# A gate group's projection as products over both parts of u, with its additions inside a softmax step and some steps moved

## The reference, cut to what matters

```
u    = modulate(rms_norm(x), shift, scale)
proj = u @ w_in            # split into q_m k_m v_m o_m if_m | q_a k_a v_a | g_m g_a
h_m  = sigmoid(o_m) * norm(mlstm(silu(conv(q_m, k_m)), v_m, gates))
h_a  = dilated window attention with ALiBi, 12 heads in 3 patterns, merged by softmax of log-sums
y    = sigmoid(g_m) * (h_m @ w_branch_m) + sigmoid(g_a) * (h_a @ w_branch_a)
x    = x + gate * (y @ w_out)
x    = x + gate * moe(...)     # 16 experts, top 2 of one group; then a final norm
```

## Time and profile before

| | us |
|---|---|
| median of 3 runs (lowest, highest) | 595.68 (595.04, 596.05) |
| the profiled execution, its own time | 594.85 |
| its span, first to last instruction | 593.1 |
| PE busy | 573.2 |
| DVE busy | 319.1 |
| ACT busy | 241.2 |

### The profile page before, as it was taken

How to read it: one execution, slowest core, us unless ns; L and a number is a source line. 1 busy time by engine, 2 the same in 40 slices (tenths; PEclk the granted TensorE clock), 3 DMA queues, 4 the chain that set the end, 5 groups by cost and what they waited for, 6 DMA issues and landing times.

```text
span 593.1 us, 8116 instructions
## 1 busy us (share of the span) xinstructions
PE 573.2 (97%) x3370; PEld 408.3 (69%) x3370; DVE 319.1 (54%) x487; ACT 241.2 (41%) x344; POOL 9.0 (2%) x23
## 2 busy tenths in 40 slices
PE   3999999999999999999999999999999999999995
PEld 1789978888888888999999988533534444353432
DVE  3679976776668868877847683612213030221204
ACT  5627658444455545764684335601111110111113
POOL 3001000000000000000000000000000000000000
PEclk9999999999999999999999999999999999999998
DMA  8999654666667939646688999399999999999992
GB/s 313 386 350 317 213 183 152 228 212 222 213 216 273 361 139 350 220 175 246 228 312 320 411 374 407 135 424 423 421 422 419 423 422 422 419 423 422 421 374 75
DMA packets 51577, 184.77 MB, mean 312 GB/s; under 512 B 3649, under 2 KB 3761, under 8 KB 37713
## 3 DMA queue, kind: packets, MB, share of 16 engines
q1 hardware_dynamic: 50706, 183.53, 80.3%
q10 hardware_dynamic: 704, 0.58, 0.3%
q0 software_dynamic: 128, 0.11, 0.1%
HBM read 183.16 MB, written 1.05 MB: 311 GB/s over the span
## 4 chain that ended last, share of the span: by engine, by line
PE 91%; DVE 4%; ACT 2%; DMA 1%; issue 1%; SPq 0%; ACTq 0%; DVEq 0%
PE ps L1660 20%; PE ps L1889 19%; PE ps L1682 15%; PE ps L1901 8%; PE ps L1637 8%; PE ps L1639 4%; PE ps L1935 3%; PE ps L1877 2%; DMA first_ada<-in_ada_w_dram 1%; PE ps L1911 1%; DVE lo L998 1%; PE ps L1671 1%; PE ps L1788 1%; PE ps L1773 1%; PE ps L1752 1%
## 5 line engine op out<-in xcount | busy, mean ns | idle before, releaser
L998 DVE TENSOR_TENSOR lo<-raw,hi 128x2048 fp32r<-128x2048 f32 (+1 forms) x51 | 114.4, 2249 | 38.6 <-ACT hi L641 38.2
L1889 PE MATMUL ps<-ring,xe_t 128*64 128x512 f32 x512 | 111.7, 593 | 0.0
L641 ACT CAST hi<-raw 128x2048 fp32r<-128x2048 f32 x50 | 95.0, 1912 | 30.1 <-PE ps L1660 15.6
L1889 PEld LDWEIGHTS ps<-ring,xe_t 128*64 128x64 f32 x512 | 36.5, 137 | 71.6 <-issue 71.4
L1660 PE MATMUL ps<-u_both,hi 128*128 128x256 f32 x448 | 82.1, 286 | 0.7 <-DVE lo L998 0.7
L1660 PEld LDWEIGHTS ps<-u_both,hi 128*128 128x128 f32 x448 | 69.9, 192 | 2.0 <-DVE lo L998 1.1
L1682 PE MATMUL ps<-hi,u_both 128*128 128x512 f32 x224 | 69.8, 393 | 1.3 <-DVE qk_m L1127 1.3
L1637 PE MATMUL ps<-u_both,hi 128*128 128x512 f32 x192 | 69.1, 403 | 0.0
L1660 PE MATMUL ps<-u_both,lo 128*128 128x256 f32 x224 | 63.5, 283 | 0.0
L1639 PE MATMUL ps<-u_both,lo 128*128 128x256 f32 x192 | 53.7, 280 | 0.0
L1457 DVE SCALAR_TENSOR_TENSOR he<-ps,w_slot,sg 128x512 f32<-128x512 f32 x8 | 6.0, 751 | 82.6 <-PE ps L1889 82.6
(11 more groups left out here) (350 smaller groups left out, 831.7 us busy)
## 6 DMA issues: line engine op xcount, KB each, us to landing
raw<-in_w_in_dram SPq DMA_DIRECT2D x41, 1024.0 KB, 5.4
ring<-in_w_gate_e_dram SPq DMA_DIRECT2D x32, 1024.0 KB, 17.3
ring<-in_w_up_e_dram SPq DMA_DIRECT2D x32, 1024.0 KB, 16.2
ring<-in_w_down_e_dram SPq DMA_DIRECT2D x28, 1024.0 KB, 15.8
raw<-in_ada_w_dram SPq DMA_DIRECT2D x16, 1024.0 KB, 6.0
first_ada<-in_ada_w_dram SPq DMA_DIRECT2D x16, 512.0 KB, 11.7
raw<-in_w_branch_m_dram SPq DMA_DIRECT2D x4, 1024.0 KB, 7.1
raw<-in_w_out_dram SPq DMA_DIRECT2D x4, 1024.0 KB, 9.2
```

The costliest lines, as they stand in the source:

```text
L641: nc.scalar.copy(hi[b % RING][:], src[:]).then_inc(hi_ready, 1)
L998: ins = V.tensor_tensor(lo[b % RING][:, tiles, :], src[:, tiles, :], hi[b % RING][:, tiles, :].bitcast(F32), ALU.subtract)
L1889: ins = mm(ps[bank][64 * s:64 * s + 64, :], xe_t[:, kk, col + s * SLOTS:col + (s + 1) * SLOTS], w[:, k, :], start=(kk == 0), stop=(kk == K ...
```

## The change

- WIDE takes in the kind gm (groups 17 and 18), with banks 0, 1 as its first pair. The sums go to `sig_gm`, and ACT's sigmoid then works in place there, after DVE's additions, where it read PSUM before.
- In the steps of gm (35 and 37) both pairs come ahead of the split of block s+2, on ACT and on DVE. For qa and ka the second pair stays behind it.
- Where the block before is one of SCORE_A_AT (block 35, after 34), DVE's additions of the first pair stand inside the softmax step of block 34, between a_max and the wait for a_exp. ACT's copies stay at the head of step 35.
- M_OUT_AT goes from 35 to 39.
- The adaLN pieces at 38 and 39 are gone; there are pieces at 17 and 21 instead, 16 in all as before.

```
--- before.py
+++ after.py
@@ -67,7 +67,7 @@
 NBLK = len(BLOCKS)
 BLK_IN = 2 * len(IN_GROUPS)
 AHEAD = RING - 1
-WIDE = [_g for _g, (_kind, _, _) in enumerate(GROUP_LIST) if _kind in ("qa", "ka")]
+WIDE = [_g for _g, (_kind, _, _) in enumerate(GROUP_LIST) if _kind in ("qa", "ka", "gm")]
 
 
 
@@ -80,7 +80,7 @@
 SCORE_A_AT = [28, 31, 34, 37]
 TURN_A_AT = [30, 33, 36, 39]
 VALUE_A_AT = [31, 34, 37, 40]
-M_OUT_AT = 35
+M_OUT_AT = 39
 M_TURN_AT = [BLK_IN - 2, BLK_IN - 1]
 FFN_ROWS_AT, FFN_COL_AT, SHIFT_LOGIT_AT = 43, 44, 45
 BCAST_AT = {45: 0}
@@ -89,7 +89,7 @@
 
 ADA_FIRST = 8
 ADA_REST = 16
-ADA_AT = {s: ADA_FIRST + i for i, s in enumerate([12, 14, 16, 18, 20, 22, 25, 26, 27, 29, 30, 32, 33, 36, 38, 39])}
+ADA_AT = {s: ADA_FIRST + i for i, s in enumerate([12, 14, 16, 17, 18, 20, 21, 22, 25, 26, 27, 29, 30, 32, 33, 36])}
 
 
 FIRST = ([("ada", a) for a in range(4)] + [("w", 0), ("w", 1), ("ada", 4), ("w", 2), ("ada", 5), ("ada", 6), ("ada", 7),
@@ -418,13 +418,13 @@
 
         def wide_banks(g):
 
-            return 2, 3, 0, 1
+            return (0, 1, 2, 3) if GROUP_LIST[g][0] == "gm" else (2, 3, 0, 1)
 
         def wide_out(g, c):
 
             kind = GROUP_LIST[g][0]
             j = [x for x in WIDE if GROUP_LIST[x][0] == kind].index(g)
-            return {"qa": q_a, "ka": k_a}[kind][:, 4 * j + c, :]
+            return {"qa": q_a, "ka": k_a, "gm": sig_gm}[kind][:, 4 * j + c, :]
 
         def wide_free(eng, g, pair):
 
@@ -705,14 +705,18 @@
 
             for s in range(NBLK):
                 g, _, _, end = BLOCKS[s]
+                kind, _, _ = GROUP_LIST[g]
                 if end and g in WIDE:
                     if g == WIDE[0]:
                         after(act, "u_lo1_3")
                     act.wait_ge(pair_done, WIDE.index(g) + 1)
                     copy_right(g, 0)
+                if end and kind == "gm":
+                    act.wait_ge(block_done, s + 1)
+                    copy_right(g, 1)
                 if s + AHEAD < NBLK and s + AHEAD != EARLY and s != LAST_BLOCK[24]:
                     split_hi(s + AHEAD)
-                if end and g in WIDE:
+                if end and g in WIDE and kind != "gm":
                     act.wait_ge(block_done, s + 1)
                     copy_right(g, 1)
                 if s == LAST_BLOCK[23]:
@@ -735,7 +739,10 @@
                 g, _, _, end = BLOCKS[s]
                 kind, _, _ = GROUP_LIST[g]
                 if end and evac_engine(g) == "act":
-                    act.wait_ge(block_done, s + 1)
+                    if g in WIDE:
+                        evacuated(act, g)
+                    else:
+                        act.wait_ge(block_done, s + 1)
                     first = min(x for x, (n, _, _) in enumerate(GROUP_LIST) if n == kind)
                     j = g - first
                     banks = banks_of(g)
@@ -755,7 +762,7 @@
                             view, src = dst[:, n, j * NB:(j + 1) * NB], ps[bank][:]
                         else:
                             view = dst[:, 4 * j + 2 * n:4 * j + 2 * n + 2, :]
-                            src = ps[bank][:].rearrange("p (c t) -> p c t", c=2)
+                            src = view if g in WIDE else ps[bank][:].rearrange("p (c t) -> p c t", c=2)
                         ins = A_(view, src, func)
                     ins.then_inc(evac_act, 1)
 
@@ -1105,11 +1112,14 @@
 
             for s in range(NBLK):
                 g, _, _, end = BLOCKS[s]
-                if end and g in WIDE:
+                kind, _, _ = GROUP_LIST[g]
+                if end and g in WIDE and s - 1 not in SCORE_A_AT:
                     add_halves(g, 0)
+                if end and kind == "gm":
+                    add_halves(g, 1)
                 if s + AHEAD < NBLK and s not in (1, LAST_BLOCK[24]):
                     split_lo(s + AHEAD)
-                if end and g in WIDE:
+                if end and g in WIDE and kind != "gm":
                     add_halves(g, 1)
                 if s == 0:
                     ada(5)
@@ -1290,6 +1300,8 @@
                                                     scalar=AD ** -0.5, in1=bias_a[:], op0=ALU.mult, op1=ALU.add))
                     V.tensor_reduce(am[:, 0:1], prob[:, 0:384], AX_X, ALU.max, negate=True)
                     event(V.tensor_reduce(am[:, 1:2], prob[:, 384:1152], AX_X, ALU.max, negate=True), f"a_max{h}")
+                    if BLOCKS[s + 1][3] and BLOCKS[s + 1][0] in WIDE:
+                        add_halves(BLOCKS[s + 1][0], 0)
                     after(dve, f"a_exp{h}")
                     step(V.reciprocal(am[:, 4:6], am[:, 2:4]))
                     V.tensor_scalar(prob[:, 0:384], prob[:, 0:384], am[:, 4:5], None, ALU.mult)
```

## The result

The changed kernel takes 597.53 us (median of 9 runs, 597.14 to 597.87), the kernel before, measured beside it, 595.53 (9 runs, 595.04 to 596.14). The ratio is 1.003, 95% interval 1.0021 to 1.0040: slower by 2.0 us, more than the 0.2% that a measurement tells from no change. Forecast was 597.5.

What follows compares the result with a forecast made beforehand. PE's own stream was taken to bound the kernel. Term 1 (-0.84 us) and term 2 (+2.68) summed to +1.84, moving the median from 595.68 to 597.5 us; own range 597.0 to 598.3, 8-in-10 range 595.8 to 598.8.

Steps and rivals of the forecast that it cites:

- What bounds: Whole kernel: PE's own stream bounds it, so what PE gains or loses in blocks 34 to 41 reaches the end one to one.
- Term 1: Four wide gm blocks: 0.347 us per product pair, 0.21 us gained a block, 0.84 us in all.
- Term 2: Before block 36: PE waits 2.49 us for banks 0 and 1, plus 0.19 restart, a loss of 2.68 us.
- The upper bound's 0.3: Hand-over before block 36: three hand-overs between engines at 0.3 us instead of 0.04 make term 2 at most about 3.4 us.
- Behind a_prob they would come 1.2 us later: DVE's additions of the first pair, if left behind a_prob instead of inside the softmax step, would come 1.2 us later.
- The second pair, the splits, head 3: Blocks 36 to 40: second pair has 1.1 us to spare, lo of block 40 1.0 us; no wait at 38 or 40.
- h_m and the pieces: h_m at 39 costs 0 with 1.2 us spare; adaLN pieces at 17 and 21 cost 0 to 0.1 us at block 24.
- The one on the other side: Rival: the pair is summed before block 36 needs its banks, only term 1 stays, 594.8 us, not slower; chance 0.12.
- The falling clock: Rival: PE's 2.5 us standstill drops the clock to 1.2 GHz for block 36, 11.1 instead of 5.55 us, 603; chance 0.03.

Runs made afterwards that it cites:

- the kernel with the first pair early: Changed kernel with ACT's copies of group 17's first pair ahead of head 2's exponentials and DVE's additions ahead of the maxima: 595.67 us against 595.64 for the kernel before.
- the two best kernels: Changed kernel, both pairs' copies ahead of the exponentials, a one-column exponential before them: 595.03 us; the same with hi of block 37 made in step 34: 594.65.
- The version without waits: Changed kernel with both pairs' copies ahead of the exponentials, a one-column exponential before them, and hi of block 37 made in step 34: 594.65 us, ratio 0.9988.
- both pairs early: Changed kernel with ACT's copies of both pairs ahead of the exponentials and DVE's additions moved forward too: 596.66 us against 595.64 for the kernel before.
- the kernel with the moves alone: Changed kernel with gm out of WIDE again, h_m kept at 39 and adaLN pieces at 17 and 21: 595.73 us against 595.64 for the kernel before.
- the repeat: Second timing of the changed kernel with DVE's additions of group 17's first pair back behind a_prob: 598.13 us against 595.49 for the kernel before.

## Why the prediction was right

The reason was right: a new wait for the first pair's banks before block 36, at the order of ACT's program. The total was right too, 597.5 against 597.53, but that it fits to the hundredth is luck. The two terms missed by 0.20 and 0.18 in opposite directions, and the slowdown, 2.0 us instead of 1.84, started from 595.53 in this set instead of 595.68. By its steps:

- **What bounds.** A shift of 1.89 us in blocks 34 to 37 came out as 2.0 at the end; the kernel with the first pair early and the two best kernels show the same in the other direction. Nothing behind took it up.
- **Term 1, -0.84.** Mis-sized by 0.20. The two-block row gave 0.347 a pair. In the changed kernel blocks 34 and 37 run at 0.347 and blocks 35 and 36 at 0.353 (from 258.69 to 259.04 in the timeline above, and on through block 36). That makes 22.4 us for 64 pairs against 23.04 for the narrow form: -0.64. The version without waits confirms it: -0.61. The slower pace was there to be read in the kernel before: in block 13 the 14 pairs between these two rows take 0.353 each, and blocks 12 to 15, 18 and 19 all run so, while rows 5 came from two of the faster blocks:

```profile
106.32 0.40 PE L1637 MATMUL ps<-u_both,hi 128*128 128x512 f32 x1
...
111.26 0.40 PE L1637 MATMUL ps<-u_both,hi 128*128 128x512 f32 x1
```

- **Term 2, +2.68.** It measured 2.50, 0.18 less. The chain was right link by link. With all times shifted by the later start (0.98), a_max should have ended at 258.70 and did at 258.71, ACT should have been free at 260.28 and was at 260.28, PE should have gone at 261.78 and went at 261.83. Three small errors: DVE to PE takes 0.15 here, not 0.04 (0.05 and 0.06 at the waits of the kernels with the first pair and with both pairs early); the restart costs 0.07, not 0.19; and block 35, at the slower pace, ended 0.1 later, so that much of the chain was hidden behind it. So a tenth that term 1 lacks comes back in term 2 by the same cause; the restart's 0.12 is chance. The upper bound's 0.3 for a hand-over has no row: the longest in this chain is the 0.15.
- **"Behind a_prob they would come 1.2 us later".** It was 0.5 (2.80 against 2.27 in the timelines of PE), less than half of that. I had put a_prob's length on top, but it runs beside ACT's copies.
- **The second pair, the splits, head 3.** No wait appeared at block 36's middle or at blocks 37, 38 and 40. The spare 1.1 us for the second pair was real: DVE's additions ended at 263.41, and PE wanted the banks half a block after 261.83, 1.3 us later. Nor was there a wait at block 24.
- **h_m and the pieces.** Cost 0 to 0.05, as said, and shown by the kernel with the moves alone; that the pieces guard h_m is shown by the 1.1 us wait. The spare time of h_m was 3.5 us, not 1.2: the forecast had the transposes near 295.4, about where they stood before, and left out that they come later with the rest.
- **The rivals.** The one on the other side decided where I had put it, at the order of ACT's program: with both pairs early and the table load out of the way the time is 594.65 to 595.03, and 594.8 was its price. The falling clock is real, but with the size off: I had it at 5.5 us and as a new time for the kernel. It is about 1.4 us in some executions of kernels with such a wait, and the nine of the changed kernel, 597.14 to 597.87, have none that stands out.

## What to carry to other kernels

When a bank must be handed over, follow the chain to the engine whose program order puts the copy behind something that waits; moving the last link (here DVE's additions) gains little while the link before it (ACT's copies behind the exponentials) sets the time. Before an instruction is put into another engine's idle time, look what already lives there: a table load of 1.28 us that my forecasts had left out came to light when its cover was taken, and the next buffer in line (lo of block 37) paid. A form that saves an instruction in three but streams the same columns is worth 0.1 to 0.2 us a block here, and all four blocks together less than one missed hand-over.

## What was not expected of the hardware

- The granted clock fell to 0.50 (1.2 GHz) for part of block 36, around a wait of PE of 2.3 us in one profile (it began to fall before PE went on) and after one of 2.8 in another, and did not in three others with the same waits (the changed kernel, the one with the pieces at 38 and 39, and the repeat). The Trainium skill (TensorE: Matmul & The Clock Gate, Why this matters for your kernels) warns of idle gaps longer than these. Here the clock fell beside shorter ones at times; no other stretch between the start and the end of the twelve profiles shows a fall, so the wait is the likely cause, but no experiment shows it.
- The pair of products has two paces at full clock, 0.3465 and 0.353 us, 2% apart. Blocks 12 to 23 show the same pattern in every profile: 12 to 15, 18 and 19 slow, 16, 17 and 20 to 23 fast. In block 34 it is fast and in 35 slow each time that gm is wide; block 36 is slow in all but one profile, and block 37 is either. What sets it stays open: it is not PE's program, which is the same in the kernels where block 37 differs, as those edits touch ACT and DVE alone.
